# Split operands in the first expert matrices of a mixture-of-experts stage

## What is computed

```
a = jnp.einsum('td,edf->tef', t, w1)
c = jnp.einsum('td,edf->tef', t, w3)
act = jax.nn.silu(a) * c * gates[:, :, None].astype(t.dtype)
y = jnp.einsum('tef,efd->td', act, w2)
```

## Time and profile before

| | |
|---|---|
| median of 3 runs | 3149.86 us (3143.45 to 3153.78) |
| the profiled execution | 3154.74 us, its span 3152.6 us |
| TensorE busy | 2931.8 us (93% of the span) |
| VectorE, ScalarE, POOL busy | 1464.6, 868.5 and 1490.7 us |
| mean granted TensorE clock | 0.960 |

### The profile page before, as it was taken

One profiled execution on the slowest core, in us unless ns is written; L12 is line 12 of the kernel. 1 busy time (PEld: TensorE's weight loads), 2 busy tenths in 40 slices (PEclk: granted clock), 3 DMA queues, 4 the chain that ended last, 5 costly groups with the idle time before them and its releaser, 6 DMA issues. The chain is left out here.

```text
span 3152.6 us, 34903 instructions
## 1 busy us (share of the span) xinstructions
PE 2931.8 (93%) x12524; PEld 2185.4 (69%) x12524; DVE 1464.6 (46%) x2176; ACT 868.5 (28%) x1615; POOL 1490.7 (47%) x920
## 2 busy tenths in 40 slices
PE   7989999999999899999999599899999798899996
PEld 5778787888877777878888467676444566675443
DVE  4865644443138656444431565644211565642213
ACT  2533323221035233232210314431111315331112
POOL 4543366666765433666666343674112245651121
PEclk9999999999999999999999799899999899989998
DMA  4221122333322211223333121144880321236842
GB/s 138 73 66 54 54 75 78 95 98 96 94 87 74 67 49 59 74 74 95 98 95 99 60 75 59 54 163 164 314 324 13 130 62 46 77 153 248 312 153 80
DMA packets 84722, 337.14 MB, mean 107 GB/s; under 512 B 18288, under 2 KB 21104, under 8 KB 76016
## 3 DMA queue, kind: packets, MB, share of 16 engines
q1 hardware_dynamic: 67600, 302.80, 29.5%
q0 software_dynamic: 15264, 26.26, 2.5%
q10 hardware_dynamic: 1728, 6.29, 0.5%
HBM read 370.93 MB, written 30.41 MB: 127 GB/s over the span
## 5 line engine op out<-in xcount | busy, mean ns | idle before, releaser
L179 POOL TENSOR_SCALAR wh<-ring 128x1024 fp32r<-128x1024 f32 x348 | 378.1, 1087 | 1100.7 <-PE ps L244 931.1
L181 POOL TENSOR_TENSOR wl<-ring,wh 128x1024 fp32r<-128x1024 f32 x348 | 848.7, 2439 | 29.0
L242 PE MATMUL ps<-xh,wh 128*128 128x512 f32 x1760 | 719.7, 409 | 68.8 <-PEq L680 22.6
L243 PE MATMUL ps<-xl,wh 128*128 128x512 f32 x1760 | 697.6, 396 | 0.0
L244 PE MATMUL ps<-xh,wl 128*128 128x512 f32 x1760 | 696.8, 396 | 0.0
L242 PEld LDWEIGHTS ps<-xh,wh 128*128 128x128 f32 x1760 | 338.8, 192 | 162.3 <-issue 57.4
L243 PEld LDWEIGHTS ps<-xl,wh 128*128 128x128 f32 x1760 | 338.4, 192 | 74.7 <-issue 6.3
L244 PEld LDWEIGHTS ps<-xh,wl 128*128 128x128 f32 x1760 | 337.6, 192 | 73.4
L1992 PE MATMUL ps<-ew,xgT 128*128 128x512 f32 x736 | 323.8, 593 | 5.5 <-ACT xgT L2195 3.5
L1992 PEld LDWEIGHTS ps<-ew,xgT 128*128 128x128 f32 x736 | 139.3, 190 | 181.1 <-issue 176.7
L1328 DVE SCALAR_TENSOR_TENSOR taps<-ps,par,taps 128x511 f32<-128x511 f32 x192 | 143.9, 749 | 250.3 <-ACT taps L1095 235.0
(11 more groups left out here) (437 smaller groups left out, 4642.6 us busy)
## 6 DMA issues: line engine op xcount, KB each, us to landing
ring<-in_w SPq DMA_DIRECT2D x348, 512.0 KB, 3.6
ew<-in_ew SPq DMA_DIRECT2D x32, 2048.0 KB, 8.2
ew<-in_ew SPq DMA_DIRECT2D x32, 1024.0 KB
yg<-ypicks SPq DMA_DIRECT2D x16, 512.0 KB, 7.1
xrows<-xr ACTq DMA_DIRECT2D x8, 512.0 KB, 2.6
z<-in_x SPq DMA_DIRECT2D x4, 512.0 KB, 9.3
gw<-in_gw SPq DMA_DIRECT2D x2, 1024.0 KB, 6.0
out<-z SPq DMA_DIRECT2D x8, 256.0 KB, 2.9
```

The costliest lines, as they stand in the source:

```text
L179: nc.gpsimd.tensor_scalar(hi, raw, 1.0, 0.0, ALU.mult, ALU.add).then_inc(sem["w_hi"], 1)
L181: nc.gpsimd.tensor_tensor(lo, raw, hi, ALU.subtract).then_inc(sem["w_split"], 1)
L242: nc.tensor.matmul(out, wh, xh, start=first, stop=False, **kw)
L243: nc.tensor.matmul(out, wh, xl, start=False, stop=False, **kw)
```

## The change

The up matrices are multiplied as split operands. ScalarE writes the high part of each quarter of an expert's up matrices (128 x 1024) into one of seven slots (`ew_h`, in the place of `xh` and `xl`), and VectorE writes the low part over the matrix itself (`ew_l` is the same memory as `ew`). Three quarters of tile j+1 come at the head of tile j on both engines, the fourth at its end. The turned rows are split as well: ScalarE writes two high halves, VectorE two low halves. An up product is 24 fp32r matmuls in four parts that wait for their quarters. The load of the up matrices is asked for by itself, after the up products of the tile that used the buffer. The code of POOL is unchanged. Some semaphores are merged (`f1_mm` and `f2_mm` into `f_mm`, `r_a` and `r_b` into `r_max`, and so on), which is left out below.

```diff
+UP_PARTS = EW_UP // D
+HI_SLOTS = 7
...
-        xgT = at_("xgT", 164, [P, C8, P])
+        ew_l = at_("ew_l", 80, [P, EW_BUFS, EW_UP + EW_DOWN], F32R)
+        ew_h = at_("ew_h", 0, [P, HI_SLOTS, D], F32R)
+        xgT_h = at_("xgT_h", 164, [P, C8, P], F32R)
+        xgT_l = at_("xgT_l", 28, [P, C8, P], F32R)
...
-                    for j in range(EXPERTS - EW_BUFS):
-                        sp.wait_ge(sem["dn_mm"], at("dn_mm", j + 1))
-                        load_expert(j + EW_BUFS)
+                    for j in range(EXPERTS - EW_BUFS + 1):
+                        if j + EW_BUFS < EXPERTS:
+                            sp.wait_ge(sem["up_mm"], at("up_mm", UP_PARTS * (j + 1)))
+                            load_up(j + EW_BUFS)
+                        if j:
+                            sp.wait_ge(sem["dn_mm"], at("dn_mm", j))
+                            load_down(j - 1 + EW_BUFS)
...
                     def expert_up(j):
 
                         b = j % EW_BUFS
-                        pe.wait_ge(sem["xgt_lo"], at("xgt_lo", j + 1))
-                        pe.wait_ge(sem["xgt_hi"], at("xgt_hi", j + 1))
-                        if j < EXPERTS:
-                            pe.wait_ge(sem[f"ew_up{b}"], at(f"ew_up{b}", 16 * (j // EW_BUFS + 1)))
-                        else:
-                            pe.wait_ge(sem[f"ew_sp{b}"], at(f"ew_sp{b}", 16 * ((j - EXPERTS) // EW_BUFS + 1)))
                         if j >= 2:
                             pe.wait_ge(sem["hact"], at("hact", j - 1))
-                        for k in range(C8):
-                            mm = T.matmul(ps[:, 2 + j % 2, :], xgT[:, k, :], ew[:, b, k * S:k * S + S], start=(k == 0), stop=(k == C8 - 1))
-                        mm.then_inc(sem["up_mm"], 1)
+                        for u in range(UP_PARTS):
+                            n = UP_PARTS * j + u
+                            if u % 2 == 0:
+                                pe.wait_ge(sem["xgt_lo"], at("xgt_lo", 2 * j + u // 2 + 1))
+                            pe.wait_ge(sem["e_lo"], at("e_lo", n + 1))
+                            for i in range(2):
+                                k, part = 2 * u + i, slice(i * S, i * S + S)
+                                mm = three(nc, ps[:, 2 + j % 2, :], xgT_h[:, k, :], xgT_l[:, k, :], ew_h[:, n % HI_SLOTS, part],
+                                           ew_l[:, b, k * S:k * S + S], k == 0, k == C8 - 1)
+                            mm.then_inc(sem["up_mm"], 1)
...
+                    def weights_high(j, parts):
+
+                        b = j % EW_BUFS
+                        if j < EXPERTS:
+                            act.wait_ge(sem[f"ew_up{b}"], at(f"ew_up{b}", 16 * (j // EW_BUFS + 1)))
+                        else:
+                            act.wait_ge(sem[f"ew_sp{b}"], at(f"ew_sp{b}", 16 * ((j - EXPERTS) // EW_BUFS + 1)))
+                        for u in parts:
+                            n = UP_PARTS * j + u
+                            if n >= HI_SLOTS:
+                                act.wait_ge(sem["up_mm"], at("up_mm", n - HI_SLOTS + 1))
+                            A(ew_h[:, n % HI_SLOTS, :], ew[:, b, u * D:u * D + D], ACT.Copy).then_inc(sem["e_hi"], 1)
+
                     def turn_evac(j):
 
                         act.wait_ge(sem["xgt_mm"], at("xgt_mm", j + 1))
-                        A(xgT[:, 0:4, :], ps[:, 0, :].rearrange("p (k t) -> p k t", t=P), ACT.Copy).then_inc(sem["xgt_lo"], 1)
+                        for half in range(2):
+                            A(xgT_h[:, 4 * half:4 * half + 4, :], ps[:, half, :].rearrange("p (k t) -> p k t", t=P), ACT.Copy
+                              ).then_inc(sem["xgt_hi"], 1)
...
+                    weights_high(0, range(UP_PARTS))
                     turn_evac(0)
                     for j in range(TILES):
-                        act.wait_ge(sem["up_mm"], at("up_mm", j + 1))
+                        if j + 1 < TILES:
+                            weights_high(j + 1, range(UP_PARTS - 1))
+                        act.wait_ge(sem["up_mm"], at("up_mm", UP_PARTS * (j + 1)))
                         if j:
                             act.wait_ge(sem["hact"], at("hact", j))
                         A(sil[:, :], ps[:, 2 + j % 2, 0:DE], ACT.Silu).then_inc(sem["silu"], 1)
                             turn_evac(j + 1)
                         if j:
                             y_evac(j - 1)
+                        if j + 1 < TILES:
+                            weights_high(j + 1, (UP_PARTS - 1,))
...
+                    def weights_low(j, parts):
+
+                        b = j % EW_BUFS
+                        for u in parts:
+                            n = UP_PARTS * j + u
+                            dve.wait_ge(sem["e_hi"], at("e_hi", n + 1))
+                            V.tensor_tensor(ew_l[:, b, u * D:u * D + D], ew[:, b, u * D:u * D + D], ew_h[:, n % HI_SLOTS, :], ALU.subtract
+                                            ).then_inc(sem["e_lo"], 1)
...
+                    weights_low(0, range(UP_PARTS))
                     turn_evac(0)
                     for j in range(TILES):
+                        if j + 1 < TILES:
+                            weights_low(j + 1, range(UP_PARTS - 1))
+                        if j < C8:
+                            do(V.scalar_tensor_tensor(z[:, j, :], z[:, j, :], ALPHA, spec[:, j, :], ALU.mult, ALU.add))
                         if j:
                             hidden_evac(j - 1)
...
                         if j:
                             y_evac(j - 1)
-                        if j < C8:
-                            do(V.scalar_tensor_tensor(z[:, j, :], z[:, j, :], ALPHA, spec[:, j, :], ALU.mult, ALU.add))
+                        if j + 1 < TILES:
+                            weights_low(j + 1, (UP_PARTS - 1,))
```

More of the change, by code:

```diff
@@ L1562, in _, with load_up, load_down @@
                     sp.dma_start(icnt[:, :, :], d_tab[:, a:a + w].rearrange("p (a n) -> p a n", a=PC)).then_inc(sem["tab_in"], 16)
-                    def load_expert(j):
+                    def load_up(j):
                         b, row = j % EW_BUFS, layer * ROWS_E + j * P
                         sp.dma_start(ew[:, b, 0:EW_UP], d_ew[row:row + P, 0:EW_UP]).then_inc(sem[f"ew_up{b}"], 16)
+                    def load_down(j):
+                        b, row = j % EW_BUFS, layer * ROWS_E + j * P
                         sp.dma_start(ew[:, b, EW_UP:], d_ew[row:row + P, EW_UP:]).then_inc(sem[f"ew_dn{b}"], 16)
@@ L1572, in _ @@
                     sp.dma_start(rt[:, :], d_rt).then_inc(sem["rt_in"], 16)
-                    load_expert(0)
-                    load_expert(1)
+                    for j in range(2):
+                        load_up(j)
+                        load_down(j)
                     stream_units(sp, sem, sh.ring, d_w, first_unit, layer * U2 + V_PLEG, min(layer * U2 + U2, DEPTH * U2 - RAW))
@@ L1579, in _ @@
                     sp.wait_ge(sem["xgt_mm"], at("xgt_mm", 1))
-                    load_expert(2)
+                    load_up(2)
+                    load_down(2)
                     sp.wait_ge(sem["spare_ready"], at("spare_ready", 1))
@@ L1726, in _ @@
                             T.matmul(ps[0:FH, 6, :], col("fw1", 0, FH, FEMB), emb[0:FEMB, :],
-                                     start=True, stop=True).then_inc(sem["f1_mm"], 1)
+                                     start=True, stop=True).then_inc(sem["f_mm"], 1)
                             pe.wait_ge(sem["lam_prod"], at("lam_prod", 1))
@@ L2066, in filter_sin @@
                     def filter_sin(n):
-                        act.wait_ge(sem[f"ang{n + 1}"], at(f"ang{n + 1}", 1))
-                        A(hid[0:FH, n, :], hid[0:FH, n, :], ACT.Sin).then_inc(sem[f"sin{n + 1}"], 1)
+                        act.wait_ge(sem["angle"], at("angle", n + 1))
+                        A(hid[0:FH, n, :], hid[0:FH, n, :], ACT.Sin).then_inc(sem["sine"], 1)
                     act.wait_ge(sem["pool_zero"], at("pool_zero", 1))
@@ L2268, in angles @@
                         reduce_angle(dve, nc, step, r, a, k)
-                        dve.sem_inc(sem[f"ang{n + 1}"], 1)
+                        dve.sem_inc(sem["angle"], 1)
                     def hy_taps(j):
@@ L2573, in _ @@
                                                ).then_inc(sem["pp_done"], 1)
+                    def weights_low(j, parts):
[5 more added lines that the diff above has]
+                                            ).then_inc(sem["e_lo"], 1)
                     def turn_evac(j):
-                        dve.wait_ge(sem["xgt_mm"], at("xgt_mm", j + 1))
-                        V.tensor_copy(xgT[:, 4:8, :], ps[:, 1, :].rearrange("p (k t) -> p k t", t=P)).then_inc(sem["xgt_hi"], 1)
+                        for half in range(2):
+                            dve.wait_ge(sem["xgt_hi"], at("xgt_hi", 2 * j + half + 1))
+                            V.tensor_tensor(xgT_l[:, 4 * half:4 * half + 4, :], ps[:, half, :].rearrange("p (k t) -> p k t", t=P),
```

(1 more changed line is left out.)

42 lines of the change are left out of this document (22 added, 20 removed).

## The result

The changed kernel took 3186.5 us (median of 4 runs, 3186.1 to 3186.9) beside 3151.5 for the kernel before (4 runs): ratio 1.0116, 95% interval 1.0097 to 1.0134, so 1.2% slower. The forecast was 3165 with a range up to 3188: the sign was right and the range held, but 35 us were lost where some 15 had been forecast, less than half. The profiled execution took 3186.9 with a span of 3184.8, that is 32.2 us more than the profiled execution of before (span 3152.6). These 32.2 are what the two traces can explain, against the +15.6 of the prediction's sum.

What follows compares the result with a forecast made beforehand. TensorE's matmuls were taken to set the pace. Terms: -38.7 regular tiles, +32.2 spare tiles, +12.1 starts, +10 clock = +15.6 us on the profiled 3154.7, so 3170.3, or 3165 as a median; range 3143 to 3188.

Steps and rivals of the forecast that it cites:

- Regular tiles: Tiles with loads known in advance: shorter up products gain 19.3 us a layer, 38.7 together, last tiles included.
- TensorE at 9.95: Regular tiles without z update: TensorE sets the pace at 9.95 us a tile, a gain of 1.45 each.
- VectorE's chain of 10.39 with the z update: Regular tiles 2 to 7: VectorE's queue sets a period of 10.39 us, a gain of 1.0 each.
- The second period: Second tile period of the expert stage: falls from 11.4 to 10.4 us.
- Loads: Regular tiles: up half asked for earlier, costed at nothing; if cover fails, 13 us per 0.5 us late.
- Starts: Start of the expert stage: up products later by 3.6 us in layer 1 and 8.5 in layer 0, 12.1 lost.
- The loop of the spares: Spare tiles: load, split, hidden rows and down products form a closed loop, 11.9 us without data, 21.1 with.
- Rival (2): Spare loads land soon enough, so no closed loop and all is covered: 3107 us, 3083 to 3090 with free starts; 10%.
- The loop, its price: Spare tiles: the closed loop loses 20.9 us in layer 0 and 11.3 in layer 1, 32.2 together.
- the clock: TensorE at half speed after idles at two starts and three loads with data: 2.0 us each, 10 lost.
- The periods with data: Three spare periods whose load moves data: 21.1 us each, apart from the clock's 2.0 each.
- Rival (3): Every tile: POOL's gather and scatter take turns with VectorE's subtractions, 26.6 us more, 3192 us; 10%.

Runs made afterwards that it cites:

- 6: Changed kernel with POOL's two splits for the next layer moved behind the scatter of tile 8: 3186.5 us, ratio 1.0106 to the kernel before.
- 1: Changed kernel with VectorE copying the hidden rows ahead of its three subtractions in spare tiles: 3129.1 us, ratio 0.9928 to the kernel before.
- 2: Changed kernel with spares split later, two parts ahead of the half of y and two behind: 3129.1 us, ratio 0.9926 to the kernel before.
- 5: Changed kernel with spare loads cut in three, the up matrix's two asked for a tile earlier: 3105.8 us, ratio 0.9852 to the kernel before.
- 3: Changed kernel with two useless TensorE products behind the turning in each spare tile: 3179.1 us, ratio 1.0089 to the kernel before.
- 7: Changed kernel with VectorE making the turned rows' low part after one starting subtraction, not four: 3175.8 us, ratio 1.0072 to the kernel before.
- 8: Changed kernel with early asks for spare up matrices, POOL's splits behind tile 8's scatter and VectorE's start reordered: 3093.7 us, ratio 0.9814 to the kernel before.
- 9: Changed kernel with early asks for spare up matrices, VectorE's start reordered and POOL's splits behind its last scatter: 3090.4 us, ratio 0.9797 to the kernel before.

## What the prediction had right, and the step that failed

**Regular tiles** (-35.8, with +4 for the clock at the two starts, so -31.8): measured -35.9. TensorE at 9.95 was 10.02. VectorE's chain of 10.39 with the z update was 0.3 too long: the periods are 10.08. The second period, given 10.4, is 9.7. The timeline of a tile with the update:

```profile
2204.82 0.79 PE L242 MATMUL ps<-ew_h,xgT_h 128*128 128x512 f32 x1
...
2205.42 0.69 DVE L2638 COPY y_a<-ps 128x512 f32<-128x512 f32 x1 [1.15 <-PE ps L2031]
...
2206.03 4.62 DVE L2618 TENSOR_TENSOR ew_l<-ew,ew_h 128x1024 fp32r<-128x1024 f32 x4
...
2206.99 1.14 POOL L1675 DMA_INDIRECT ypicks<-y_a,dst  x1 [3.31 <-DVE y_a L2638]
...
2210.57 0.69 DVE L2648 SCALAR_TENSOR_TENSOR z<-z,spec 128x512 f32<-128x512 f32 x1
...
2211.29 0.42 DVE L2631 COPY hactT<-ps 128x256 f32<-128x256 f32 x1
...
2214.91 0.80 PE L242 MATMUL ps<-ew_h,xgT_h 128*128 128x512 f32 x1
```

The order is the one forecast, with nothing between. Four subtractions take 4.54 up to the next start (1.135 each, where I had 1.18: 0.18 less), y's half 0.61 (0.08 less), and the rest is within 0.05 of its terms. Loads cost nothing, as said.

**Starts** (+12.1): measured +11.2. Layer 1's 3.6 came out at 3.66, layer 0's 8.5 at 7.57. I took the upper end for POOL's splits, all of 4.9; they cost 4.3, shown by 6: 8.90 us for four subtractions beside the splits, 4.63 without them. Without the splits layer 0's start would have cost 3.3.

**The loop of the spares, its form**: right at each link, and 1, 2 and 5 cut it in three places, and each time the last five periods of each layer, 12.5 and 14.2 before the cut, fall to between 10.0 and 10.6. Rival (2) had set its condition at the load, landing too late by 2 us or more; 5 meets the condition and shows 3105.8 (3101.9 to 3113.7) where the rival gave 3107.

**The loop, its price** (32.2, and 6 of the 10 for the clock): 59.6. This is the step that failed: the loop was priced with an instruction and a landing that nothing held (0.99 and 2.1), and its down products at the full clock in every period without data. The traces show 1.92 and 3.0, and the halved clock in seven of eleven. Of the 21.4:
- *POOL's instruction.* I took 0.99 and 2.1 from the earlier trace rows, where VectorE had no subtraction to make. The split's fourth part stands just where POOL asks for the load, begins 0.16 before it and holds it for the rest of its own length. That is 0.9 a period (4), of which 0.25 are covered by links that I had taken too long (the three subtractions take 3.4 and not 3.54, the hidden rows' copy and hand-off 0.48 and not 0.67): 0.65 x 11 = 7.
- *The clock in the periods without data.* I had put half speed only behind idles like that of the earlier trace rows, 7.9 us. In the loop the idle of 2.3 us was followed by the lower clock in seven periods of eleven: 1.7 x 7 = 12, shown by 3. This was to be read before the run. Idles of TensorE of 2 to 4 us have both outcomes in the trace of the kernel before, here the 3.5 us behind one of 2.16 and behind one of 3.06:

```profile
1945.28:1948.78 3.50, 3.50 (x10) 2.80 (x11) 2.16 (x3) 1.42 (x5) 0.00 (x0) 0.60 0.00 0
...
906.28:909.78 3.50, 3.50 (x15) 2.91 (x16) 0.00 (x0) 0.00 (x0) 3.35 (x2) 1.00 0.73 219
```

- *The periods with data*: 24.6, 24.4 and 22.9 for 3 x 21.1 and 6 of clock, 2.6 more. Their down products took 6.13, 5.67 and 4.72 in place of 3.14, 7.1 in all for the 6; ScalarE could begin 12.1, 12.3 and 11.8 after the start of POOL's instruction, where I had 11.3, which is 2.4; other links were shorter. This rest was not tried alone.

**Rival (3)**, VectorE and POOL taking turns in every tile, stood at 10% and 26.6 us in the regular tiles. It did not happen there, and the mechanism was at work all the same, in the spare loop. I had set against it that the earlier trace rows show a z update beside a gather, neither longer. There the gather began first, by 0.26 us. The trace of after has the other order, and it decides. The scatter of the tile shown above and that of the next one:

```profile
2216.11 3.48 DVE L2618 TENSOR_TENSOR ew_l<-ew,ew_h 128x1024 fp32r<-128x1024 f32 x3
...
2217.37 1.98 POOL L1675 DMA_INDIRECT ypicks<-y_b,dst  x1 [3.62 <-issue]
```

Subtractions in a row start 1.14 apart. The scatter at 2206.99 begins 0.2 before one ends and takes 1.14, where the shortest of its line takes 0.97; the second begins 0.1 after the next one (2216.11 + 1.14 = 2217.25) and takes 1.98. What POOL loses is the rest of the subtraction that runs when it begins. In the trace of after, 51 gathers, scatters and loads begin while such a subtraction runs, with 0.17 to 1.05 of it left; less that rest they take 0.86 to 0.99, where a free one takes 0.97 to 1.02. Another 30 begin while VectorE makes the low part of the turned rows, which has one input in PSUM, with 0.5 left; these take 0.99 to 1.02 and are not held. The Trainium skill (SBUF — State Buffer, "SBUF: two separate sides") has it that of a VectorE operation with two SBUF inputs and a GpSimd one that reads SBUF the one that starts first has the shared ports for the whole instruction and the other fully blocks. The traces agree where the subtraction began first, with the rest of an instruction of 1.2 us as the most that one hold costs here. They do not where the gather, scatter or load began first: the z update of the earlier trace rows took 0.68 all the same, and the subtractions behind the two scatters above keep their distance of 1.14. In regular tiles the same hold meets a scatter that has slack, in the spare tiles a load that has none.

**What an open loop shows of the change itself.** With the loop open (5) the change is worth -47.6 us against the kernel before, where rival (2) had -43 with the starts as they are. The 80.7 us between 5 and the changed kernel (81.6 by the stages) hang on when the spares' transfers are asked for.

## What to carry to other kernels

Where a step is put between a transfer and its use, ask first what releases the transfer: if its release waits, through any queue, for something that stands behind the new step, the latency of the transfer is in every turn, and shortening the products changes nothing. Then cut the loop at the cheapest place, here an ask one tile earlier or one copy moved ahead. Work that moves away from one conflict takes its price along unless it goes to a place where the other engine has no two-input work: look for such a place first.

## What the runs showed of the hardware that I had not expected

- A halved clock after short idles, and not each time. An idle of 2.3 us before the down products was followed by a granted clock of 0.64 over the next 4.8 us, in seven of eleven periods; with the idle filled by useless products (3) ten of the eleven had down products of 3.14, the time at 1.00. At a stage's start the same order, ending in an idle of 1.4 us, was followed by 1.00 twice and by 0.56 or 0.57 over 3.5 us three times (7, 8, 9).
- A POOL instruction that only issues an indirect transfer is held by a VectorE subtraction with both inputs in SBUF, from 0.99 to 1.9 us, and the transfer lands as much later (2.1 to 3.0). The instruction does not hold the subtraction in turn. POOL's own splits do, and both sides lose: the longest of 184 subtractions took 3.36 us, 1.22 alone, and a split's two operations 2.02 and 3.19 us, 1.06 and 2.35 alone.
- The DMA engines were 0.93 busy, at 350 GB/s, for 140 us, and no engine waited for a load in that time (5).
